# One stage for a layer's output projection, network and gate, and a block's maximum ahead of the preceding block's mixture

## The reference

```python
m = diff_attention(...) if i % 2 else neighborhood_attention(...)   # ends in o @ w_o
x = x + rms_norm(m, g[1])
f = conv_glu_ffn(rms_norm(x, g[2]), w_in, conv_w, conv_b, w_out)
x = x + rms_norm(f, g[3])
gate = sigmoid(rms_norm(x, g[4]) @ ple_w_gate)
x = x + gate * (p[i] @ ple_w_proj)
```

## Time and profile before

| | |
|---|---|
| median of 3 runs | 2433.63 us (2433.51 to 2435.15) |
| the profiled execution | 2435.52 us, span 2433.7 us |
| PE busy | 2239.7 us (92%) |
| DVE busy | 1298.5 us (53%) |
| ACT busy | 915.4 us (38%) |
| POOL busy | 141.6 us (6%) |
| mean granted PE clock | 0.961 of full speed |

### The profile page before, as it was taken

The page is one execution under the profiler, slowest core; times in us unless marked ns, Lnnn a source line. Parts: engine busy times, 40 slices in busy tenths (PEclk is TensorE's granted clock), DMA queues, the critical chain, the costliest instruction groups (busy, mean ns, idle before and its releaser), DMA issues. The chain is left out here.

```text
span 2433.7 us, 35815 instructions
## 1 busy us (share of the span) xinstructions
PE 2239.7 (92%) x14010; PEld 1764.7 (73%) x14010; DVE 1298.5 (53%) x1697; ACT 915.4 (38%) x1432; POOL 141.6 (6%) x113
## 2 busy tenths in 40 slices
PE   6998999999888989799999989998877589999999
PEld 5786788888666666678888867777857436788887
DVE  5554576653466666466665356683434564533333
ACT  4434432222444555542222255552211343423322
POOL 0000011110000000001110000001322110000000
PEclk9998999999999999999999999999978879999999
DMA  6230233333222221213333322330000002333332
GB/s 224 96 122 27 70 113 95 95 104 95 78 76 89 67 68 34 62 60 117 95 99 96 96 72 80 87 93 21 4 2 3 13 1 69 96 97 100 96 95 69
DMA packets 52584, 186.97 MB, mean 77 GB/s; under 512 B 5712, under 2 KB 5968, under 8 KB 52336
## 3 DMA queue, kind: packets, MB, share of 16 engines
q1 hardware_dynamic: 52176, 184.69, 24.4%
q10 hardware_dynamic: 288, 0.58, 0.1%
HBM read 183.15 MB, written 2.10 MB: 76 GB/s over the span
## 5 line engine op out<-in xcount | busy, mean ns | idle before, releaser
L263 PE MATMUL ffn_banks<-ffn_r_hi,ffn_w_hi 128*128 128x512 f32 x1056 | 412.7, 391 | 2.1 <-DVE ffn_r_lo L376 1.5
L265 PE MATMUL ffn_banks<-ffn_r_hi,ffn_w_lo 128*128 128x512 f32 x1056 | 410.9, 389 | 0.0
L264 PE MATMUL ffn_banks<-ffn_r_lo,ffn_w_hi 128*128 128x512 f32 x1056 | 410.9, 389 | 0.0
L263 PEld LDWEIGHTS ffn_banks<-ffn_r_hi,ffn_w_hi 128*128 128x128 f32 x1056 | 198.2, 188 | 46.9 <-DVE ffn_r_lo L376 3.3
L264 PEld LDWEIGHTS ffn_banks<-ffn_r_lo,ffn_w_hi 128*128 128x128 f32 x1056 | 198.3, 188 | 41.5 <-issue 0.7
L265 PEld LDWEIGHTS ffn_banks<-ffn_r_hi,ffn_w_lo 128*128 128x128 f32 x1056 | 198.2, 188 | 41.1
L242 ACT ACTIVATE ffn_w_hi<-ring 128x1024 fp32r<-128x1024 f32 x132 | 138.6, 1055 | 215.6 <-PE ffn_banks L265 213.7
L248 DVE TENSOR_TENSOR ffn_w_lo<-ring,ffn_w_hi 128x1024 fp32r<-128x1024 f32 x132 | 197.6, 1498 | 27.6 <-ACT ffn_w_hi L242 24.3
L263 PE MATMUL ff_banks<-ff_r_hi,ff_w_hi 128*128 128x512 f32 x512 | 200.0, 391 | 0.0
L265 PE MATMUL ff_banks<-ff_r_hi,ff_w_lo 128*128 128x512 f32 x512 | 199.2, 389 | 0.0
L264 PE MATMUL ff_banks<-ff_r_lo,ff_w_hi 128*128 128x512 f32 x512 | 199.2, 389 | 0.0
(11 more groups left out here) (504 smaller groups left out, 4205.9 us busy)
## 6 DMA issues: line engine op xcount, KB each, us to landing
ring<-weights SPq DMA_DIRECT2D x315, 512.0 KB, 3.6
na_bias<-window_bias SPq DMA_DIRECT2D x16, 512.0 KB, 5.6
da_rel<-t_rel SPq DMA_DIRECT2D x8, 448.0 KB, 4.6
X<-xT SPq DMA_DIRECT2D x1, 2048.0 KB, 3.2
outT<-X SPq DMA_DIRECT2D x8, 256.0 KB, 2.5
const<-consts SPq DMA_DIRECT2D x1, 1328.5 KB, 14.3
ple_pt<-pT SPq DMA_DIRECT2D x2, 512.0 KB, 3.6
H<-lora ACTq DMA_DIRECT2D x1, 384.0 KB, 2.9
```

The lines of the kernel that those rows point to most:

```text
L263: pe.matmul(psum, hi, self.r_hi[:, rhs_slot, :], start=start, stop=False)
L264: pe.matmul(psum, hi, self.r_lo[:, rhs_slot, :], start=False, stop=False)
L265: return pe.matmul(psum, lo, self.r_hi[:, rhs_slot, :], start=False, stop=stop)
```

## The change

In the differential attention DVE takes the bias and the maximum of block n ahead of the reciprocal and the mixture of block n - 1, and ACT scales n - 1 after it has rounded the chunk and copied the weights of n - 2, directly ahead of the exponentials of n.

The stages "wo", "ffn" and "ple" of a layer become one, `layer_tail`. The first chunk of the embedding's projection moves in the weight stream from behind the network to ahead of it, and PE makes these 24 products between the output projection and the network, the other 24 between the network and the gate. The embedding is loaded at the start of the stage and rounded and split twice. The filler products ahead of the network go; those ahead of the output projection stay, and the first load of an activation table there stands behind the first weight roundings. The sum of the output projection's squares is made by four products by ones, three of them inside the last tile; the sum of the network's by four, two ahead of and two behind the first projection tile; the later sum in the gate by one in place of four. At the end of the network ACT squares all eight tiles and copies four out, DVE copies the other four and adds pairs of squares. In each norm one weight split stands between DVE's fourth and fifth tile. The buffers of the gate lie in the tiles of the network's middle. The third block's stage (`up_down`) keeps its form and loses the cases that it no longer needs.

```diff
                 for n in range(NBLK + 1):
-                    if n:
-                        invert(n - 1)
-                        mix(n - 1)
                     if n == 0:
                         for c in chunks_of(0):
                             evacuate(c)
...
                     if n < NBLK:
                         add_bias(n)
+                    if n:
+                        invert(n - 1)
+                        mix(n - 1)
                     if n >= 13 and n % TT == 1:
                         norm((n - 13) // TT)
                 for c in range(blocks_before(NBLK - 1) // DT, N):
...
                 for n in range(NBLK + LAG_O):
-                    if 0 < n <= NBLK:
-                        scale_half(n - 1)
                     if n < NBLK:
                         for c in chunks_of(n):
                             round_ahead(c)
                     if 0 <= n - LAG_T < NBLK:
                         weights_out(n - LAG_T)
+                    if 0 < n <= NBLK:
+                        scale_half(n - 1)
                     if n < NBLK:
                         exponentials(n)
...
+    WO, PA, UP, DOWN, PB, GATE = 0, DT, DT + 1, DT + 1 + 2 * FT, DT + 1 + 3 * FT, DT + 2 + 3 * FT
+    N = GATE + DT
...
+        down_bank = [4, 5, 6, 7, 0, 1, 2, 3]
+        pa_bank = [4, 5, 7, 0]
+        pb_bank = [5, 6, 7, 0]
+        gate_bank = [1, 2, 3, 5, 6, 7, 0, 1]
...
+                def wo_tile(j):
+                    if j >= 4:
+                        pe.wait_ge(s["wo_out"], j - 3)
+                    weights(j)
+                    for b in range(DT):
+                        if j == 0:
+                            pe.wait_ge(sp_.rhs_split, b + 1)
+                        mm = sp_.multiply(pe, banks[:, j % 4, :], j, b, b, b == 0, b == DT - 1)
+                        if j == DT - 1 and b == 3:
+                            for pair in range(3):
+                                pe.wait_ge(s["wo_gathered"], pair + 1)
+                                pe.matmul(banks[:, 6, :], k.c("ones"), k.H[:, 2 * pair, :], start=pair == 0, stop=False)
+                    mm.then_inc(k.chunk_done, 1)
...
+                keep_busy(pe, k, banks[:, 3, :], 4)
+                for j in range(DT):
+                    wo_tile(j)
+
+                weights(PA)
+                pe.wait_ge(s["pt_split"], PLE_T)
+                project_embedding(PA, 0, pa_bank[0], "pa_done")
+                pe.wait_ge(s["wo_gathered"], 4)
+                pe.matmul(banks[:, 6, :], k.c("ones"), k.H[:, 6, :], start=False, stop=True).then_inc(s["summed"], 1)
+                project_embedding(PA, 1, pa_bank[1], "pa_done")
+                project_embedding(PA, 2, pa_bank[2], "pa_done")
+                pe.wait_ge(s["wo_out"], 5)
+                project_embedding(PA, 3, pa_bank[3], "pa_done")
+
+                pe.wait_ge(s["pa_out"], 2)
+                pe.wait_ge(s["wo_out"], DT)
+                first_tiles(UP, 0, up_bank)
+                pe.wait_ge(s["pa_out"], 4)
+                up(0, 3, free=False, between=lambda: mean_square(7, 1))
...
+                pe.wait_ge(s["m_low"], 1)
+                for pair in range(2):
+                    pe.wait_ge(s["out_gathered"], pair + 1)
+                    pe.matmul(out(0), k.c("ones"), k.H[:, 2 * pair, :], start=pair == 0, stop=False)
+                weights(PB)
+                pe.wait_ge(s["pt_split"], 2 * PLE_T)
+                pe.wait_ge(s["m_low"], 2)
+                project_embedding(PB, 0, pb_bank[0], "pb_done")
+                for pair in range(2, 4):
+                    pe.wait_ge(s["out_gathered"], pair + 1)
+                    mm = pe.matmul(out(0), k.c("ones"), k.H[:, 2 * pair, :], start=False, stop=pair == 3)
+                mm.then_inc(s["summed"], 1)
+                pe.wait_ge(s["m_low"], 4)
+                project_embedding(PB, 1, pb_bank[1], "pb_done")
+                project_embedding(PB, 2, pb_bank[2], "pb_done")
+                pe.wait_ge(s["m_high"], 4)
+                project_embedding(PB, 3, pb_bank[3], "pb_done")
+
+                first_tiles(GATE, 1, lambda j: banks[:, gate_bank[j], :])
                 for f in range(FIRST, DT):
-                    pe.wait_ge(scaled, f - 3) if f >= 4 else pe.wait_ge(proj_out, 6)
-                    pe.wait_ge(k.chunk_split, g0 + PLE_T + f + 1)
+                    if f < DT - 1:
+                        pe.wait_ge(s["pb_out"], f - FIRST + 1)
+                    else:
+                        pe.wait_ge(s["pre_done"], 1)
+                    weights(GATE + f)
                     for b in range(DT):
-                        mm = sp_.multiply(pe, acc[:, f % 4, :], PLE_T + f, b, b, b == 0, b == DT - 1)
-                        if f == FIRST and b == 1:
-                            for j in range(4):
-                                pe.wait_ge(gathered, j + 1)
-                                sums = pe.matmul(ms[:, 1, :], k.c("ones"), k.H[:, 2 * j, :], start=j == 0, stop=j == 3)
-                            sums.then_inc(summed, 1)
+                        mm = sp_.multiply(pe, banks[:, gate_bank[f], :], GATE + f, b, slot(1, b), b == 0, b == DT - 1)
+                        if f == FIRST and b == 5:
+                            pe.wait_ge(s["lned"], 3)
+                            mean_square(4, 2)
...
                 sp_.round_chunk(act, 0, 0)
+                for j in range(DT):
+                    sp_.round_rhs(act, k.H[:, j, :], j)
                 for c in (1, 2, 3):
                     sp_.round_chunk(act, 0, c)
+                act.preload_act_table_set(LN_EXP)
+                act.wait_ge(s["pt_loaded"], 16)
+                round_embedding(DT)
                 for j in range(DT):
+                    chunk_done(act, j)
+                    act.activation(k.H[:, j, :], banks[:, j % 4, :], ACT.Square).then_inc(s["wo_squared"], 1)
+                    act.activation(m[:, j, :], banks[:, j % 4, :], ACT.Copy).then_inc(s["wo_out"], 1)
+                    sp_.round_chunk(act, 0, j + SLOTS)
+                root(6, 1, "r1_done")
+                embedding_out(0)
+                embedding_out(1)
+                for j in range(DT):
+                    normed(0, j)
+                    if j in (1, 2):
+                        embedding_out(j + 1)
+                    if j == 3:
+                        sp_.round_chunk(act, 0, UP + 3)
+                sp_.round_chunk(act, 0, UP + 4)
+                root(7, 2, "rstd_done")
...
+                act.preload_act_table_set(LN_EXP)
+                for o in range(DT):
+                    out_done(act, o)
+                    act.activation(k.H[:, o, :], out(o), ACT.Square).then_inc(s["out_squared"], 1)
+                for o in range(4, DT):
+                    act.activation(m[:, o, :], out(o), ACT.Copy).then_inc(s["m_high"], 1)
+                sp_.round_chunk(act, 0, GATE + 2)
+                embedding_out(4)
+                root(4, 3, "r1_done")
+                embedding_out(5)
+                for j in range(DT):
+                    normed(1, j)
+                    if j < 2:
+                        embedding_out(6 + j)
+                    if j == 3:
+                        sp_.round_chunk(act, 0, GATE + 3)
+                sp_.round_chunk(act, 0, GATE + 4)
+                root(4, 4, "rstd_done")
...
+                def post_norm(norm, third):
+                    dve.wait_ge(s["r1_done"], norm + 1)
+                    for j in range(DT + 1):
+                        if j < DT:
+                            dve.scalar_tensor_tensor(out=m[:, j, :], in0=m[:, j, :], scalar=k.p(gains[norm][0], j), in1=k.rstd[:, :],
+                                                     op0=ALU.mult, op1=ALU.mult).then_inc(s["scaled"], 1)
+                            dve.wait_ge(s["scaled"], DT * norm + j + 1)
+                            dve.tensor_tensor(k.X[:, j, :], k.X[:, j, :], m[:, j, :], ALU.add).then_inc(s["added"], 1)
+                        if j:
+                            lo(norm, j - 1)
+                        if j == 4:
+                            sp_.split_chunk(dve, 0, third + 1)
+                    for j in range(1, DT):
+                        dve.wait_ge(s["squared"], DT * norm + j + 1)
+                        if j > 1:
+                            dve.wait_ge(s["gathered"], (DT - 1) * norm + j - 1)
+                        dve.tensor_tensor(k.H[:, 0, :], k.H[:, 0, :], k.H[:, j, :], ALU.add).then_inc(s["gathered"], 1)
+                    sp_.split_chunk(dve, 0, third + 2)
+                    dve.wait_ge(s["rstd_done"], norm + 1)
...
+                def copy_out(o):
+                    dve.wait_ge(s["out_squared"], o + 1)
+                    dve.tensor_copy(m[:, o, :], out(o)).then_inc(s["m_low"], 1)
+
+                def gather(pair):
+                    dve.wait_ge(s["out_squared"], 2 * pair + 2)
+                    dve.tensor_tensor(k.H[:, 2 * pair, :], k.H[:, 2 * pair, :], k.H[:, 2 * pair + 1, :], ALU.add).then_inc(s["out_gathered"], 1)
+
```

(25 more changed lines are left out.)

446 lines of the change are left out of this document (199 added, 247 removed).

## The result

The changed kernel takes 2374.63 us in the median (2372.33 to 2380.48, four runs) against 2433.57 before; the ratio is 0.9761, with a 95% interval of 0.9742 to 0.9779. Its profiled execution took 2374.99 us, its span is 2373.2. So 60.5 us of span went, where the prediction had 44.4.

A forecast was written before the change was run, and what follows sets the result against it. PE was taken to be at its pace inside stages, losing time at seams and in the attention's DVE-ACT chain. Seams 27.1 and attention 17.3 us off the 2433.63 median gave 2389.3 us; range 2378 to 2404 (8 in 10).

The forecast's parts named there:

- the likeliest case: Whole kernel: the seams' and the attention loop's gains come about as priced, 2380 to 2397 us, chance 0.70.
- seams, four: Output projection to network gains 4.3 and 4.0 us, network to gate 9.6 and 9.2, in layers 0 and 1: 27.1.
- loop, intervals without a split (8), less PE's holds: Attention: 8 plain intervals gain 1.54 us each, 12.3, less 2 for PE's transposition waiting for the mixture.
- loop, with a split (11): Attention intervals with a weight split: only 0.5 us gained each, as DVE now waits for ACT's rounding; 5.5 in all.
- loop, with a head's output or root (6): Attention split intervals following a head's output or reciprocal root on ACT: these still stand before the rounding, gain 0.
- loop, last six: Attention's last six intervals, no splits left: PE busy 38.40 of 41.94 us, so at most 3.5 gained, 3 taken.
- behind the last maximum: Attention's end: last block's exponentials start 0.8 us later, its scaling behind one more copy (0.7): a loss of 1.5.
- The loop's lower bound of 3 us: Attention: if waits for the rounding are 2 us, not 1.0, nothing of the 19 blocks' gain is left: 3.
- It gives nothing: Output projection's start: moving ACT's table load behind the first weight rounding gives nothing, at most 1.3 us; four fillers stand ahead.
- Rival D: Slower: PE's clock falls in the attention; 2432 us at a mean clock of 0.80, 2448 at 0.75; chance 0.05.
- Rival C: All goes: attention reaches PE's busy time and seams their bound, 24.4 + 32 us, giving 2377; chance 0.05.
- all that PE idles there: Attention loop's upper bound: PE busy 199.73 of 224.17 us, so at most 24.4 us can be gained.

The follow-up runs named there:

- the halved projection: Changed kernel with half of the embedding's projection left out, 3 products per tile in place of 6: 2372.71 us, one run; tails 473.0 and 471.8 us.
- the experiment: Kernel before with only the output projection's first activation-table load moved behind the first rounding: 2433.76 us against 2434.36, ratio 0.9996.
- the other two kernels with that stage: Kernel before with only the attention's new DVE and ACT orders, 2407.26 us; kernel before with only the first table load moved, 2433.76 us.
- the small edits: Edits to the changed kernel, such as DVE's attention split behind the maximum (2372.83 us), or that with fewer products by ones and the norm's split moved (2375.04 us).
- four edits: Changed kernel with attention splits behind the maximum, fewer products by ones at the first seam, norm's split behind the tiles, two fillers: 2368.27 us against 2375.53.

## Why the prediction came out short

The seams' mechanism and price were right, the loop's mechanism was; the sum was 16.1 us too small, and the time lies 3.4 us below the range and 5.4 below the likeliest case (2380 to 2397). The steps that failed are the loop's price (17.3 us with its end, 25.3 measured) and three terms put at nothing: the start of layer 0, the start of the attention and the third block (8.7 us together). Each term, from the trace of before and the first one after:

| term | priced | measured |
|---|---|---|
| seams, four | 27.1 | 26.7 |
| loop, intervals without a split (8), less PE's holds | 10.3 | 12.8 |
| loop, with a split (11) | 5.5 | 6.7 |
| loop, with a head's output or root (6) | 0 | 2.15 |
| loop, last six | 3 | 3.2 |
| behind the last maximum | -1.5 | 0.4 |
| start of layer 0 | 0 | 3.1 |
| start of the attention to its first maximum | 0 | 0.7 |
| third block | 0 | 4.9 |
| all else | 0 | -0.2 |

*Seams: right.* 8.0 and 10.3 us to the first product (7.7, 10.1), waits of 1.20 and 0.98 (1.2), full clock at the second. A tail gave 13.6 and 13.1 us (13.9 and 13.2). The chain at the first seam came 0.3 us dearer than priced, and the split in the middle cheaper: 0.73 and 0.75 us, not 1.15. That the chain and not PE sets the seams is shown by the halved projection.

*Loop: right in kind, too small by 6 us.* The terms that failed: "8 plain" intervals at 1.54 each took the first for one of them. Between the first two maxima no mixture stands any more, since there is no block before the first. Timeline of DVE:

```profile
739.15 1.22 DVE L1226 TENSOR_REDUCE da_nmax<-da_e 128x2 f32<-128x1024 f32 x1
740.46 1.23 DVE L1223 TENSOR_TENSOR da_e<-da_s_ps,da_rel 128x1024 f32<-128x1024 f32 x1
741.72 1.22 DVE L1226 TENSOR_REDUCE da_nmax<-da_e 128x2 f32<-128x1024 f32 x1
```

It is 2.57 us (5.77 before), 1.7 more than priced. PE's holds cost less than the 2 us set against the plain intervals: the other seven gained 9.6 us where 1.54 each is 10.8, so some 1.1 went to them; in four of the seven DVE waits 0.5 to 1.4 us for PE's scores. A split interval is 6.83, not 7.0, and 11 of them make 1.2. The intervals with a head's output or root gained 0.3 to 0.5 each, "gain 0" was their price: DVE waits 1.2 to 2.2 us for the rounding in them, and why just that much is left was not tried. The loop's lower bound of 3 us does not follow from its sentence either: one more microsecond of waiting in each of 11 split intervals leaves some 6 of the 17.3.

*Behind the last maximum: wrong.* The last block's exponentials start later, but PE has other work there; the stretch from the last maximum to the fillers shrank by 0.4 where 1.5 was charged.

*Start of layer 0: two things.* "It gives nothing" failed for the table load: four fillers last 3.5 us, the chain with the load 4.4, so 0.9 us came free, shown by the experiment. The other 2.2 are the clock: the fillers of the profiled execution of before ran at half clock, those of the other two kernels with that stage at full. The prediction subtracted from that one execution, and had no row for this start.

*Third block: not in the prediction.* It says nothing on a block that no edit touches. In fourteen traces its length has three values: 931.1 to 931.8 us in nine of them (all three with the old stages, and six of eleven with the new one), 926.7 to 927.0 in three, 923.3 and 923.4 in two. The granted clock of its middle goes with them: 0.85 or 0.86, 0.88, and 0.89. The trace of the changed kernel that the table is from has the middle value, so 4.9 of the 60.5 us come from a block that no edit touches. Without them the span would be 2378.1, at the lower end of the range. Yet they are more than one trace's luck. The changed kernel's execution with the long value took 2378.09 us, and its three medians are 2374.63, 2373.13 and 2375.53; of the kernel before no execution on record lies as much as 4.9 us under its median (one of ten does with the table load moved, 2428.81). So the shorter values seem to come with the new stage (in traces five in eleven against none in three). That is read from whole times and few traces, and why it should be so stays open. The three lengths do explain why the small edits that won 4 us and more did not show in medians of four: executions of one kernel differ by up to 8 us.

Rival D fell: the loop is granted 1.00, more than before, with four transpositions in each block. The Trainium skill's rule that transposes don't count as busy ("TensorE: Matmul & The Clock Gate", Part 4: PE-mode transpose) shows in nothing here; the test is a weak one, since transposes are some 15 of 120 us of PE's records between 780 and 900 us. Rival C (2377, all goes) was nearest in time, but its seams (32) did not come. Its loop did, 24.85 us against "all that PE idles there", 24.4, though PE still idles 6.35 us: that bound was none. PE's busy time in the loop was 199.73 us at a clock of 0.98 and is 192.97 at 1.00. An estimate: a mean of 0.98 over 224.17 us is some 9 us at the lower level, whose work takes 4.5 us less at the upper one; the remaining 2 are not shown, shorter records where fewer products wait inside would be a reason.

## What to carry to other kernels

In a software pipeline over two engines, order an engine's program so that what waits for the other engine stands behind independent work of its own; then look for the next hand-over, here the rounding behind the exponentials, and fill that wait too until the matrix engine is the bound. Price the first and the last turns of a loop by themselves, for they lack a neighbour. Subtract from several executions where a stretch in the trace is at a mixed clock. Compare small edits by their stretches, the untouched ones too: the whole time can hide 4 us behind a clock that an untouched block is granted, and a third of what four edits won went back that way.

## What the runs showed of the hardware

- The same instructions of the third block's middle take 223.3 to 223.4, 226.7 to 227.0 or 231.1 to 231.8 us, at a mean granted clock of 0.89, 0.88 or 0.85 to 0.86, with nothing between in fourteen traces.
- Waits of 3.25 and 3.21 us ahead of the network were followed by a granted clock of 0.76 and 0.90 over 14 us, one of 1.20 at the same place by 1.00; a wait of 3.04 us ahead of layer 0's gate was followed by 1.00 as well.
- At a granted clock of 1.00 a full-precision product by ones of 128 x 512 takes 0.86 us of PE, a product of a rounded and a rest part 0.227.
- ACT's table load at layer 0's start before is a record of 1.28 us, and moving it off the chain gave 0.9 us, what the fillers did not cover.
